# Reading a matmul's moving columns, and writing its results, from the last to the first

## What is computed

```
h = rmsnorm(x);  proj = h @ w_in                  # 2048 x 7184
x += concat(stick_breaking(...), gated_delta(...)) @ w_out
x += cross_attention(rmsnorm(x), rmsnorm(mem)) @ w_xo
u = causal_dwconv(rmsnorm(x) @ w_up) + b;  x += (silu(gate) * up) @ w_down
x = rmsnorm(x)
p = rmsnorm(x) @ fox_w_in;  x += (fox_attention(...) * silu(gate)) @ fox_w_out
p = rmsnorm(x) @ swa_w_in;  x += (window_attention(...) * silu(gate)) @ swa_w_out
return rmsnorm(x)
```

## Time and profile before

| | |
|---|---|
| median of three runs | 2169.99 us (2169.81 to 2170.38) |
| span of the profiled execution, first to last instruction | 2167.6 us |
| TensorE matmuls busy | 2156.3 us, 99% |
| TensorE weight loads busy (beside the matmuls) | 1865.8 us, 86% |
| VectorE busy | 1618.3 us, 75% |
| ScalarE busy | 1327.2 us, 61% |
| DMA | 180 GB/s on average |

### The profile page before, as it was taken

One profiled execution on the slowest core, in us unless ns is written; L12 is line 12 of the kernel. 1 busy time (PEld: TensorE's weight loads), 2 busy tenths in 40 slices (PEclk: granted clock), 3 DMA queues, 4 the chain that ended last, 5 costly groups with the idle time before them and its releaser, 6 DMA issues.

```text
span 2167.6 us, 34503 instructions
## 1 busy us (share of the span) xinstructions
PE 2156.3 (99%) x13406; PEld 1865.8 (86%) x13406; DVE 1618.3 (75%) x2945; ACT 1327.2 (61%) x2601; POOL 9.7 (0%) x22
## 2 busy tenths in 40 slices
PE   9999999999999999999999999999999999999998
PEld 8888888888888888888888888888888888888887
DVE  7898666786688877655778867777676767688774
ACT  7866447775576666544666656555556655567764
POOL 0000000000000000000000000000000000000000
PEclk9999999999999999999999999999999999999999
DMA  7443434665455555555555555545554455544453
GB/s 279 169 146 137 147 115 141 218 217 186 156 190 189 188 191 186 193 185 192 187 191 189 185 194 185 193 171 197 181 177 174 167 192 186 189 161 155 146 200 140
DMA packets 107619, 389.31 MB, mean 180 GB/s; under 512 B 12304, under 2 KB 12560, under 8 KB 106688
## 3 DMA queue, kind: packets, MB, share of 16 engines
q1 hardware_dynamic: 105264, 377.31, 50.2%
q0 software_dynamic: 1904, 9.47, 1.2%
q10 hardware_dynamic: 288, 0.32, 0.0%
HBM read 384.34 MB, written 2.13 MB: 178 GB/s over the span
## 4 chain that ended last, share of the span: by engine, by line
PE 95%; DVE 3%; ACT 1%; issue 0%; DMA 0%; SPq 0%; DVEq 0%; ACTq 0%
PE main L510 88%; PE two L510 6%; PE two L513 1%; DVE WL L987 1%; DVE gt L987 0%; DMA RAW<-ws 0%; DVE GQ L993 0%; ACT L1654 0%; ACT WH L1655 0%; DVE GK L993 0%; PE main L556 0%; ACT PP L1655 0%; DVE PB L987 0%; ACT NT L1655 0%; DVE PP L993 0%
## 5 line engine op out<-in xcount | busy, mean ns | idle before, releaser
L1655 ACT ACTIVATE WH<-RAW 128x512 fp32r<-128x512 f32 x1416 | 882.1, 629 | 657.6 <-PE main L510 651.1
L987 DVE TENSOR_TENSOR WL<-RAW,WH 128x512 fp32r<-128x512 f32 x1416 | 961.2, 687 | 383.9 <-ACT WH L1655 374.4
L510 PE MATMUL main<-A,WH 128*128 128x512 f32 (+1 forms) x3680 | 1141.9, 393 | 1.0 <-DVE WL L987 1.0
L510 PEld LDWEIGHTS main<-A,WL 128*128 128x128 f32 x3584 | 673.9, 188 | 154.8
L510 PE MATMUL main<-A,WL 128*128 128x256 f32 x3584 | 713.7, 278 | 0.0
L510 PEld LDWEIGHTS main<-A,WH 128*128 128x128 f32 x3680 | 562.7, 189 | 13.8 <-issue 9.3
L510 PE MATMUL main<-H,WH 128*128 128x512 f32 x704 | 221.1, 395 | 0.0
L510 PE MATMUL main<-B,WH 128*128 128x512 f32 (+1 forms) x640 | 184.4, 373 | 0.0
L510 PEld LDWEIGHTS main<-H,WL 128*128 128x128 f32 x704 | 132.3, 188 | 31.3
L510 PE MATMUL main<-H,WL 128*128 128x256 f32 x704 | 138.4, 278 | 0.0
L510 PE MATMUL main<-WH,A 128*128 128x512 f32 (+1 forms) x448 | 137.6, 380 | 0.0
(11 more groups left out here) (322 smaller groups left out, 1722.5 us busy)
## 6 DMA issues: line engine op xcount, KB each, us to landing
RAW<-ws SPq DMA_DIRECT2D x707, 512.0 KB, 3.3
CB<-cscr POOLq DMA_DIRECT2D x4, 1024.0 KB, 4.7
XT<-xT POOLq DMA_DIRECT2D x4, 512.0 KB, 6.0
MS<-memT POOLq DMA_DIRECT2D x4, 512.0 KB, 8.7
xs<-xT SPq DMA_DIRECT2D x7, 256.0 KB, 7.6
out<-YT SPq DMA_DIRECT2D x7, 256.0 KB, 2.6
CST<-cst SPq DMA_DIRECT2D x1, 1248.0 KB, 7.9
G<-g POOLq DMA_DIRECT2D x1, 1024.0 KB, 5.9
```

The source lines that it names most:

```text
L510: return e.matmul(o, l, r, start=start, stop=True, skip_group_check=True)
L987: return e.tensor_tensor(o, a, b, op)
L1655: return e.activation(o, i, f, bias=bias, scale=scale, accum_out=accum)
```

## The change

A second helper, `back`, turns two operands round: the moving operand is read from its last column to its first, and the output is written from its last column to its first. Column k of the moving operand still ends up in column k of the output. All matmuls of the weight stream use it; the stationary operands and all matmuls outside the stream (outputs in `two`, and the transposes with which each "w2" chunk begins) stay as they are. The slices have step -1, so the access pattern starts at the last element and counts down; no instruction, wait or buffer is added, taken away or moved.

```diff
+            def back(o, l, r, start=True):
+                return mm(o[:, ::-1], l, r[:, ::-1], start)
+
...
                         for t in range(2):
-                            mm(P[:, t, :], h[:, cols[t]], both, start=first and r == 0)
+                            back(P[:, t, :], h[:, cols[t]], both, start=first and r == 0)
                         for t in range(2):
-                            ins = mm(P[:, t, 0:T], l[:, cols[t]], hi, start=False)
+                            ins = back(P[:, t, 0:T], l[:, cols[t]], hi, start=False)
...
                             hi, lo = (X[:, kt, a, 128 * t:128 * t + 128] for a in range(2))
-                            mm(P[:, t, 0:n], hi, h[:, cols], start=first and r == 0)
-                            mm(P[:, t, 0:n], hi, l[:, cols], start=False)
-                            ins = mm(P[:, t, 0:n], lo, h[:, cols], start=False)
+                            back(P[:, t, 0:n], hi, h[:, cols], start=first and r == 0)
+                            back(P[:, t, 0:n], hi, l[:, cols], start=False)
+                            ins = back(P[:, t, 0:n], lo, h[:, cols], start=False)
...
-                        mm(o, h[:, cols], X[:, kt, 0, :], start=first and (r == 0 if form == "small" else r % 2 == 0))
-                        mm(o, l[:, cols], X[:, kt, 0, :], start=False)
-                        ins = mm(o, h[:, cols], X[:, kt, 1, :], start=False)
+                        back(o, h[:, cols], X[:, kt, 0, :], start=first and (r == 0 if form == "small" else r % 2 == 0))
+                        back(o, l[:, cols], X[:, kt, 0, :], start=False)
+                        ins = back(o, h[:, cols], X[:, kt, 1, :], start=False)
```

More of the change, by code:

```diff
@@ L576, in main @@
                             kh, kl = (W[:, (j - i + kt) % NW, :] for W in (WH, WL))
-                            mm(P[:, t, :], hi, kh, start=False)
-                            mm(P[:, t, :], hi, kl, start=False)
-                            ins = mm(P[:, t, :], lo, kh, start=False)
+                            back(P[:, t, :], hi, kh, start=False)
+                            back(P[:, t, :], hi, kl, start=False)
+                            ins = back(P[:, t, :], lo, kh, start=False)
                         if i == n - 1 and t == 0:
```

## The result

Turned reads and writes make the kernel slower: 2196.82 us median of four runs against 2170.03, ratio 1.0124 with a 95% interval of 1.0109 to 1.0138, 26.8 us. The profiled execution took 2197.37 us with a span of 2195.6; the one of before, 2167.6.

What follows compares the result with a forecast made beforehand. TensorE, taking stream matmuls back to back, was taken as the bound. The span of 2167.6 + 0 (columns) + 0 (starts) us, with the runs' median 2.4 us above it, gave 2170 us; range 2162 to 3985.

Steps and rivals of the forecast that it cites:

- What bounds the kernel: TensorE's matmuls, busy 2156.3 of 2167.6 us, set the weight stream's pace; VectorE has 75%, ScalarE 61%.
- Price of a column: Each stream matmul column keeps 0.4167 ns when the address counts down, a change of 0 us.
- rival 2: Half rate: PSUM's write port or the moving operand's read port pairs only rising addresses; around 3850 us, chance 0.24.
- the float32 row: Plain float32 products ahead of "xo0", read as 209 ns per 256 columns, taken as upper bound of 0.816 ns a column.
- Price of a start: Each stream matmul's fixed part stays about 14 ns whichever end it begins at, a change of 0 us.
- Rival 1: A stream matmul's start costs one to two cycles more, 4.7 to 9.3 us; around 2180 us, chance 0.11.
- Rival 3: Faster: turning the order shortens a wait within the 14 ns of stream matmuls; not under 2012 us, chance 0.07.
- the likeliest case: No change in the whole kernel's time, 2170 us, own range 2166 to 2175; chance 0.58.
- What would show it: Trace signs: unchanged matmul distances if right; the same few ns at 256 and 512 columns for a changed start price.

Runs made afterwards that it cites:

- bench1: TensorE alone, blocks of 48 float32r matmuls, length, places and directions varied; 512 columns took 226.8 ns forward, 233.4 with both turned.
- bench3: TensorE alone, everything forward, first column of moving or stationary operand varied; 512 columns took 226.6 ns with both shifted by 8 columns.
- bench2: TensorE alone, outputs forward, the read's length, first column and direction varied; 320 columns took 146.6 ns in either direction.

## Why the prediction was right or wrong

- *What bounds the kernel*: right. TensorE's added time is the kernel's added time, nothing hid any of it, and no other engine came near the bound (VectorE 74%).
- *Price of a column*: right for the rate of one per cycle; the half rate of rival 2, to which I gave 0.24, was nowhere. The bound that I had made of the float32 row was an answer to another question, and I misread the row: the code has 8 such matmuls (two for each of four heads), so the 16 records are two for each, and 256 columns cost 418 ns, not 209. The merging of neighbours in a line was my argument for no change. The write side agrees with it (zero within 0.1%), but no run shows that this is why.
- *Price of a start*: this is the step that failed. "I take 14 ns, a change of 0 us." It is 20 ns in the tokens form, 16.7 in the wide one and 11.7 in the plain one. The argument was that nothing in a start depends on the end at which it begins. The runs showed that what is not columns depends on the first column's place, above all against the stationary operand, and forward too: between about 13 and 23 ns with 512 columns. With 512 columns a downward read pays 20 at every place tried alone. The three forms had nearly the same 14 ns before, and I took that for a constant; all operands of the stream start at multiples of 512 bytes from one base, so the trace of before held only one place (bench1 to bench3 vary it).
- *Rival 1* had the sign and, in its stretch to 2328 us, the size; its likeliest 2180 was 17 us short. I counted one or two cycles, and it was 6 on average, 16 in the tokens form. Its mechanism, a fetch that goes further for every turned matmul, is wrong: 256 columns alone got cheaper, and with 320 columns there is no difference.
- *Rival 3* fell as an effect of direction, but not as a possibility: part of the 14 ns can be had back, by 64 or 192 bytes of placement, 8 us.
- *Numbers*: 2196.8 lies in the range of 2162 to 3985 by luck: the range reached that far only for the half rate, which did not come. It is outside the likeliest case's own range of 2166 to 2175. Slower had 0.35, no change 0.58; the forecast itself missed by 26.8 us. I had written that one cycle per matmul is 0.21%, and should have read from it that "the same within 0.2%" asks for a start equal to a cycle over 11,168 matmuls; that deserved less than 0.58.
- *What would show it*: I asked for "the same few ns at 256 and at 512 columns". It was not the same: 6.5 ns more at 512 columns in tokens, and in the wide form, by the starts of neighbours, 2 ns less from the first 512 to the second, 0 from 256 to 256, and 5 to 7 more at the two changes of length. That was the first sign of a phase.

One sentence of the Trainium skill bears on the explanation. "TensorE: Matmul & The Clock Gate", Step-by-step: what each phase is for, says that the two operands have independent read ports and loading the next weights doesn't take bandwidth from the running matmul. Here 226.6 ns become 233.2 or 233.4 by a shift of 8 columns of either operand alone (L48, L72 and L128 of bench3), so they are not independent in time, whatever the port.

## What to carry to other kernels

Where TensorE is the bound and takes matmuls back to back, what each costs beyond its columns is worth a look: here 7% of the kernel, and it depends on where the moving operand starts against the stationary one, in steps of 32 bytes with a period of 256. Try the placements (an offset of 32 to 224 bytes on one buffer) with a bench of TensorE alone before the kernel, since it gave the kernel's distances within 2 ns for four matmuls. Reading 512 columns backward had the price of a bad place wherever it was tried, so it costs most where the forward read stands well; writing backward to PSUM was free.

## What the runs showed of the hardware

- Two prices come back again and again for 512 columns, 226.7 and 233.3 ns, which are 544 and 560 cycles at 2.4 GHz; other placements lie between or a little above. With 256 forward it is 120.0 ns, 288 cycles. Why 16 cycles, no run shows.
- The mean price of 512 columns forward depends on the moving operand's place: 226.6 at 0 (L48), 233.2 at 8 (L72), 226.6 at 64 (L114), by the rows above. With 256 columns forward, by whole blocks of bench3: 121.7 ns at 0 (L50), 127.5 at 2 (L56), 115.6 at 4 (L62).
- The part beyond the columns is not the same at every length: 128 and 192 columns both take about 112 ns (bench2, L46 and L50: 5.31 and 5.42 us for 48), 320 take 146.6, which is again 13 ns beyond the columns.
- A stationary operand of 32 columns does not make the next matmul come sooner: 231.8 ns against 226.7 with 128 columns.
